# PE multiplies the identity with itself at the borders between stages of a diffusion trunk

## The reference

```python
def peer_ffn(h, w_q, keys, u_tab, v_tab):
    q = (h @ w_q).reshape(bn, t, PEER_HEADS, 2, PEER_HALF)
    s = jnp.einsum('bthcd,hckd->bthck', q, keys)
    s_top, i_top = lax.top_k(s, PEER_TOPK)
    ...
    best_s, pos = lax.top_k(cand_s, PEER_TOPK)
    gates = jax.nn.softmax(best_s, axis=-1)
    ...
        pre = jnp.einsum('ced,cd->ce', jnp.take(u_tab, ii, axis=0), hh)
        act = jax.nn.gelu(pre, approximate=False)
        return jnp.einsum('ce,ced->cd', act * gg, jnp.take(v_tab, ii, axis=0))

for i in range(DEPTH):
    x = x + mx[2] * mixer(modulate(rms_norm(x, norm1_g[i]), mx[0], mx[1]))
    x = x + mx[5] * peer_ffn(modulate(rms_norm(x, norm2_g[i]), mx[3], mx[4]), ...)
return rms_norm(x, final_g)
```

## Time and profile before

| what | value |
|---|---|
| median of 3 runs | 4153.09 us (4151.8 to 4156.67) |
| profiled execution, span | 4139.5 us |
| PE busy | 3881.7 us, 94% |
| DVE busy | 3194.6 us, 77% |
| ACT busy | 1963.3 us, 47% |
| POOL busy | 1169.6 us, 28% |
| TensorE's mean granted clock | 0.973 |
| bytes moved | 1026 MB, 248 GB/s |

### The profile page before, as it was taken

How to read it: one execution, slowest core, us unless ns; L and a number is a source line. 1 busy time by engine, 2 the same in 40 slices (tenths; PEclk the granted TensorE clock), 3 DMA queues, 4 the chain that set the end, 5 groups by cost and what they waited for, 6 DMA issues and landing times. The chain is left out here.

```text
span 4139.5 us, 63328 instructions
## 1 busy us (share of the span) xinstructions
PE 3881.7 (94%) x20946; PEld 3333.0 (81%) x20946; DVE 3194.6 (77%) x5918; ACT 1963.3 (47%) x3786; POOL 1169.6 (28%) x905
## 2 busy tenths in 40 slices
PE   8998988999999989999997999778899999899998
PEld 2787877788888868888886777657899999899997
DVE  2698789999997768888886555658998877677777
ACT  2212234777777722222223555433488887333333
POOL 0232212343443334444442222123122222122221
PEclk9999999999999999999999999979999999999999
DMA  7443116899999999999991111022589898899996
GB/s 295 163 162 113 46 54 216 305 326 334 331 341 339 334 358 372 375 373 377 373 373 60 55 46 46 31 77 66 183 299 308 308 309 312 306 333 332 333 332 219
DMA packets 411884, 1026.09 MB, mean 248 GB/s; under 512 B 33968, under 2 KB 182448, under 8 KB 405680
## 3 DMA queue, kind: packets, MB, share of 16 engines
q1 hardware_dynamic: 296496, 604.22, 41.5%
q0 software_dynamic: 110592, 402.70, 26.8%
q10 hardware_dynamic: 4608, 16.78, 1.1%
HBM read 904.03 MB, written 119.54 MB: 247 GB/s over the span
## 5 line engine op out<-in xcount | busy, mean ns | idle before, releaser
L136 ACT ACTIVATE w_hi<-w_raw 128x1024 fp32r<-128x1024 f32 x536 | 568.3, 1060 | 1174.1 <-PE psum L1428 881.9
L168 PE MATMUL psum<-h_hi,w_hi 128*128 128x512 f32 (+1 forms) x2208 | 853.0, 386 | 89.6 <-PEq L809 32.8
L170 PE MATMUL psum<-h_hi,w_lo 128*128 128x512 f32 (+1 forms) x2208 | 832.5, 377 | 0.0
L169 PE MATMUL psum<-h_lo,w_hi 128*128 128x512 f32 (+1 forms) x2208 | 832.3, 377 | 0.0
L147 DVE TENSOR_TENSOR w_lo<-w_raw,w_hi 128x1024 fp32r<-128x1024 f32 x424 | 519.4, 1225 | 387.2 <-ACT w_hi L136 366.7
L1426 PE MATMUL psum<-a_hie,w_hi 128*128 128x512 f32 (+1 forms) x2048 | 756.6, 369 | 31.0 <-DVE a_loe L1499 31.0
L1428 PE MATMUL psum<-a_hie,w_lo 128*128 128x512 f32 (+1 forms) x2048 | 756.7, 369 | 0.0
L1427 PE MATMUL psum<-a_loe,w_hi 128*128 128x512 f32 (+1 forms) x2048 | 754.1, 368 | 0.0
L1298 POOL DMA_INDIRECT u_rowsg<-in_peer_u_rows,expert_idx x384 | 446.1, 1162 | 1050.9 <-DVE u_rowsg L1053 919.4
L1407 POOL DMA_INDIRECT v_rowse<-in_peer_v,expert_idx x384 | 421.1, 1097 | 830.1 <-DVE row_sume L1508 816.9
L1228 ACT ACTIVATE ojg<-eq_jg,gate_Tg 128x128 fp32r<-128x128 bf16 x1792 | 550.2, 388 | 109.9 <-DVE eq_jg L1076 109.4
(11 more groups left out here) (263 smaller groups left out, 5474.5 us busy)
## 6 DMA issues: line engine op xcount, KB each, us to landing
w_raw<-in_peer_u SPq DMA_DIRECT2D x256, 512.0 KB, 6.0
w_raw<-in_peer_v SPq DMA_DIRECT2D x256, 512.0 KB, 5.4
gates<-stageg SPq DMA_DIRECT2D x28, 2048.0 KB, 15.9
acts<-act_gg SPq DMA_DIRECT2D x128, 256.0 KB, 5.1
gte<-gates SPq DMA_DIRECT2D x32, 1024.0 KB, 8.3
act_fe<-acts SPq DMA_DIRECT2D x128, 256.0 KB, 6.0
ada_w<-in_ada_w SPq DMA_DIRECT2D x12, 2048.0 KB, 8.7
ada_rows<-in_ada_w SPq DMA_DIRECT2D x48, 512.0 KB, 3.8
```

Source lines behind the costliest of these rows:

```text
L136: act.activation(self.weights(s)[0], self.raw[:, slot, :], ACT.Copy).then_inc(self.hi_done, 1)
L168: pe.matmul(out, wh, hi[:, k], start=(k == 0), stop=False)
L169: pe.matmul(out, wh, lo[:, k], start=False, stop=False)
L170: last = pe.matmul(out, wl, hi[:, k], start=False, stop=(k == KC - 1))
```

## The change

A method `keep_busy(pe, bank, count)` issues `count` products of the identity (`ident`, 128 x 128, f32) with four copies of itself side by side (512 columns), into one PSUM bank that nothing reads at that time. It is called at seven points of the program: ahead of the first tile of `stage_rank` (9 times in layer 0, 4 in layer 1), at the end of `stage_rank` (13 in both layers), at the end of `stage_gates` (14 and 11), and at the end of `stage_experts` in layer 0 (14). That makes 78 products. At the end of `stage_rank` and of `stage_gates` a wait stands ahead of them, for the engine that reads bank 7.

```diff
+    def keep_busy(self, pe, bank, count):
+
+        for _ in range(count):
+            pe.matmul(self.psum[:, bank, :].rearrange("p (a x) -> p a x", x=P), self.ident[:],
+                      self.ident[:].unsqueeze(1).to_broadcast([P, 4, P]), start=True, stop=True)
...
                     last.then_inc(s_mm, 1)
+                t.keep_busy(pe, 5, 9 if tokens == TOK else 4)
                 for k in range(KC):
                     norm.ready(pe, k)
                     t.product(pe, 0, 0, t.moving(tokens), [k])
...
                     scores(i, i)
+                pe.wait_ge(h_tok_done, S)
+                t.keep_busy(pe, 7, 13)
...
                         t.product(pe, c, c % SPLIT, moving, [k], c % W)
+                pe.wait_ge(oh_ready, dense * GB)
+                t.keep_busy(pe, 7, 14 if layer == 0 else 11)
...
                     total(KC + d, sq_rows[:, d % 2].rearrange("p s x -> p (s x)"), sums[:, Td:tokens])
+                if layer == 0:
+                    t.keep_busy(pe, 7, 14)
```

## The result

The changed kernel took 4181.78 us (median of 4 runs, 4180.47 to 4186.69), the kernel before 4152.44 in the same comparison (4 runs, 4150.44 to 4156.67): ratio 1.0079, 95% interval 1.0067 to 1.0092, so 28 to 38 us more. The direction was forecast, the size wasn't: 15.3 us was the sum of the steps, and 4179 the top of the range. The profiled execution has a span of 4181.3 us and took 4183.0, so here 1.7 us lie around the span. The 13.6 us of the profile before were thus not overhead but an execution that happened to be short.

The account below looks back on a forecast made before the run. TensorE's clock was full in nearly every slice, so only gaps at stage borders and the half-clock bursts after them were open. Terms -2.2 + 2.8 + 2.7 + 12.0 = +15.3 us on 4153.1 gave 4168.4 us, range 4159 to 4179.

Parts of the forecast that it names:

- A border waits for PE's arithmetic: At stage ends: the next stage starts 0.24 us after PE's modelled end, so fillers outlasting other engines delay it by their excess.
- (4): End of `stage_gates`, layer 0, 14 fillers: they outlast their cover, cost 2.8 us; clock low again at the next product, gain 0.
- The first rival: At stage ends: the border doesn't wait for queued products, so not slower; 4150.9 or 4143.4 us, chance 0.08.
- (1): Start of `stage_rank`, layer 0, 9 fillers: clock high for the first tile, but PE doesn't bound it; gain 0.
- (2): Start of `stage_rank`, layer 1, 4 fillers: they fit within the 7.17 us gap and DVE paces the tile; gain 0.
- (3): End of `stage_rank`, layer 0, 13 fillers: border stays, clock holds, 4.42 us burst takes 2.21; gain 2.2 us.
- (5): End of `stage_rank`, layer 1, 13 fillers: 3.6 to 6.6 us idle afterwards, so the clock falls; gain 0, or 2.7 us if held.
- (6): End of `stage_gates`, layer 1, 11 fillers: they outlast their cover, cost 2.7 us; then 7.0 us idle, clock low, gain 0.
- (7): End of `stage_experts`, layer 0, 14 fillers: all on the path, cost 12.0 us; clock low again before PE's next product, gain 0.
- The low clock rival: At the fillers: they don't raise the clock, so those ending layer 0's `stage_rank` cost 7.6 us; 4178.2 us or more, chance 0.05.
- the one pass rival: At each filler: it is a single pass of 0.43 us, giving 4159.1 us; chance 0.06.
- All low-clock time counts: Across gaps and bursts: everything there runs at half pace at low clock, 56 us to get back, 4097 us; chance 0.01.

Follow-up runs that it names:

- only7: Changed kernel with only the call at the end of layer 0's `stage_experts` kept; 4155.13 us against 4146.71 for the kernel before (ratio 1.0021).
- late7: only7 with its 14 products moved behind the border, first in PE's program of the HGRN stage; 4147.92 us against 4147.14 for the kernel before (1.0002).
- realign: Changed kernel with 14 more one-column products ahead of the first added call; 4167.6 us against 4146.71 for the kernel before (1.0051).
- behind: Changed kernel with fillers moved behind borders, except those ending `stage_rank`, and 30 one-column products at the start; 4144.31 us against 4147.14 for the kernel before (0.9995).
- shift50: Kernel before plus only 50 one-column products in layer 0's `stage_rank`; 4155.85 us against 4149.03 (1.0018).
- shift64: Kernel before plus only 64 one-column products in layer 0's `stage_rank`; 4149.15 us against 4149.03 (1.0003).
- no7r: Changed kernel without its last call, the first call's 9 products replaced by 37 of one column; 4148.53 us against 4147.14 for the kernel before (1.0003).
- narrow: Changed kernel with every added product cut from 512 columns to 1; 4158.44 us against 4146.71 for the kernel before (1.0028).

## Why the prediction was right or wrong, point by point

**Price of a filler: right.** Forecast 0.86 us; 28 instructions in 12.18 us are 0.87 a filler.

**A border waits for PE's arithmetic: right,** and with it the sign. The memset behind (4) comes 2.8 us later, as forecast, and experts 0 is 12 us longer. The first rival said that PE's report would overtake its fillers; only7 against late7 rules it out, since the same 14 products cost 12 us ahead of the border and none that can be measured behind it. By the rule of the Trainium skill that this rival went with (TensorE: Matmul & The Clock Gate, Step-by-step) those two kernels would be alike; for products ahead of a border the measurement decides against that use of it. The sequencer may well run ahead; the border doesn't.

**(1), gain 0: right in the number, wrong in a step.** I had the clock high for the tile. The fillers ended at 411.44, and the clock fell again before the tile at 414.90 (the gap's mean of 0.85 puts it 2.4 us behind the fillers), so in the changed kernel the gain was 0 because the tile was as cold as before. That a warm tile gains nothing either, the reason I gave, is shown by realign (194.4 us against 193.8).

**(2), gain 0: right,** and by the reason given: 7.25 us for the same 15 products at 1.00 and at 0.60, DVE busy for 7.11 in both.

**(3), gain 2.2: wrong in its size.** I had the clock hold through the gap, which it did, and took it that it then stays high, which it didn't: it fell 0.8 us into the burst (the product at 597.27 takes 0.47 us, those from 598.34 on 0.63), and the mean is 0.61. In 4.42 us that is (0.61 - 0.50) x 4.42 = 0.5 us of work at full clock more than before. It is a sum from the clock, not a measured gain: `stage_gates` scatters by 8 us in four profiles of before, far more than 0.5. How long the clock outlived PE's end I had from gaps in which PE stayed idle; the burst that began 2.64 us after the fillers did not keep it up. In behind the same 13 fillers ended earlier, 4.32 us ahead of the burst, and its first 4.4 us ran at 0.50.

**(4), (5), (6): right.** 2.8 and 2.8 us of excess ((6) from 6.96 to 9.7 us), and (5)'s next product came 6.6 us after its fillers, cold.

**(7), cost 12.0: right,** 12.0 in after and 11.5 to 12.7 in only7.

**What failed is the sum, by a term it didn't have.** It was made of what stands at the seven borders. Its first paragraph asked what the body of a stage can gain from work in idle time, found nothing, and so put the bodies at 0; what instructions added ahead of a body can cost it was put at 0 without being asked. But the body of the HGRN stage was in play: it cost 11.3 us, of which 7.3 are idle time put down to issue (0.3 before) that comes and goes with the fetched packets. The remaining 4 fit the products at half clock behind the two pauses, which no run measured apart. With it the terms are 12.0 + 2.8 + 2.8 - 0.5 + 11.3 = 28.4 us; the two comparisons measured 28 to 38 and 24 to 35. (The surplus of `stage_gates` of layer 1, below, is not in them.) With the loop's term taken out (realign), +14 to +28 remain, which holds the forecast of 15.3. A row for this was in the profile of before, had I asked what the change adds besides time: the loop's second and third pass fetch nothing there, so it is held, and whether it still is with 200 instructions more ahead of it was a question to put.

The Trainium skill has the sizes for it (Advanced Engine Details and Errata, ISA Cache): 128 KB on TensorE, and lines of 16 KB, which are 256 instructions. The section says nothing of loops. From its sizes I estimate 8 lines for TensorE, so that a loop that touches 8 is held and one that touches 9 is not. The trace agrees with these sizes: 16.3 KB a packet, 9 packets in a pass of shift50, none in shift64. That 256 added instructions cost nothing where 200 do also fits, since the profile counts four instructions for each product of one column (63584 in shift64 against 63328 before, 256 for 64 products). How many instructions the loop has in all, and so where it lies against the lines, no run measured: the profile leaves out some kinds.

**The low clock rival and the one pass rival** are out by the rows of the fillers: two instructions each, 0.43 us apart, and at (3) the clock rose from 0.50 (to 584) to 1.00 (from 585) while nothing but fillers ran from 582.10 on. **All low-clock time counts:** behind and late7 took the low clock from bursts of the HGRN and the experts stages, and the stages stayed as long.

**What stays open.** gates 1 takes 645.5 to 646.8 us in four profiles of before and 648.8 to 654.9 in all ten with added instructions, also where none stands near it (only7, late7). Experts 1 gives part of it back in most of them (586.9 to 590.3 against 589.8 to 590.5). In late7 PE idles once for 1.85 us, behind a wait of ACT for a transfer of `act_gg`, and runs at a clock of 0.81 and 0.62 in the 6 us around it; why the transfers fall otherwise wasn't tried. The medians of no7r, late7 and shift64 stand 0.1 to 1.4 us above before, so the two stages together cost little.

## What to carry to other kernels

An instruction that is put ahead of a loop has a second price beside its time: it moves the loop against the borders of the blocks in which an engine's program is fetched. Look at the fetch queue's packets before and after, and for idle time put down to issue at a back jump; if it has appeared, some instructions more, where the engine waits anyway, can take it away. Work that is meant to be covered belongs behind a border between stages, not ahead of it, since the border waits for it; and a cold burst is only worth warming if PE bounds the tile it stands in: warmed here, none of these bursts gave a measurable gain.

## What the runs showed of the hardware

- A loop whose passes fetch nothing (no packets from 2392 to 2592) turned, with 200 instructions ahead of it, into one that fetches 9 packets of 16 KB a pass; each back jump then stalls PE for 3.5 to 3.9 us (eight jumps in four profiles). The granted clock is at 0.50 for the products behind it, in seven of the eight from the first product on, in narrow's second (2516.36) from the second. 56 instructions more took the stall away again.
- The granted clock fell within a burst of PE, 0.8 us after its start and 3.4 us after the fillers' end, though it had been 1.00 through the gap of 2.64 us ahead of it.
- A tile at full clock that waits for another engine lost the clock in its midst (realign, 1.00 to 424.00, then 0.50), so a warmed tile can be paid for in the next microseconds. It needn't: in after layer 1's tile kept 1.00 for its first 7.25 us.
- Nine profiles of kernels whose `stage_gates` of layer 0 is that of before (before four times, only7, late7, behind, shift50, shift64) show 875.3 to 885.9 us for it; a single profile tells nothing there below 10 us.
